# Tile 1's second attention: two pairs' scores and row maxima ahead of the last queries, the second eight experts behind the last pair, gates and first dots inside its end

## The reference

```python
logits = where(valid, q @ k.T / 8 + rel_bias, -1e30)        # 16 heads, 256 keys
probs  = softmax(concat([logits, sink]))[..., :-1]
x = x + (probs @ v) @ w_o
q  = (rmsnorm(x) @ w_q).reshape(tokens, 8, 2, 128)           # PEER: 8 heads, 2 halves
sv, si = top_k(q @ subkeys, 16)                              # of 128 keys, for each half
top_v, pos = top_k(sv[0][:, None] + sv[1][None, :], 16)      # 16 of 256 sums
g  = softmax(top_v);  e = index of the expert of each pos    # 128 experts a token
x = x + sum_e g_e * gelu(xn . u[e]) * v[e]
```

## Time and profile before

| | us |
|---|---|
| median of 3 runs (lowest, highest) | 1862.94 (1861.97, 1864.53) |
| time of the profiled execution | 1865.89 |
| its span, first to last instruction | 1863.7 |
| PE busy | 1628.6 |
| DVE busy | 1051.9 |
| POOL busy | 639.7 |
| ACT busy | 556.0 |

### The profile page before, as it was taken

How to read it: one execution, slowest core, us unless ns; L and a number is a source line. 1 busy time by engine, 2 the same in 40 slices (tenths; PEclk the granted TensorE clock), 3 DMA queues, 4 the chain that set the end, 5 groups by cost and what they waited for, 6 DMA issues and landing times.

```text
span 1863.7 us, 19396 instructions
## 1 busy us (share of the span) xinstructions
PE 1628.6 (87%) x6412; PEld 959.6 (51%) x6412; DVE 1051.9 (56%) x2710; ACT 556.0 (30%) x1673; POOL 639.7 (34%) x532
## 2 busy tenths in 40 slices
PE   9999999999997888888888789799888889877776
PEld 7888886976443444443443246554444444422222
DVE  3112202137656766666766654676676677676664
ACT  1211000102423333333333333433334333333432
POOL 1000000003534445344454530154444444444542
PEclk9999999999999999999999999999999999999999
DMA  9544238527999999999999995899999999999996
GB/s 250 137 120 164 101 136 302 183 91 300 415 415 421 421 421 421 414 410 417 422 418 406 421 352 205 315 402 415 418 421 421 421 421 417 422 416 418 417 419 285
DMA packets 153072, 642.57 MB, mean 345 GB/s; under 512 B 9987, under 2 KB 50067, under 8 KB 87180
## 3 DMA queue, kind: packets, MB, share of 16 engines
q0 software_dynamic: 74976, 540.92, 70.5%
q1 hardware_dynamic: 77996, 100.42, 16.2%
HBM read 640.19 MB, written 1.11 MB: 344 GB/s over the span
## 4 chain that ended last, share of the span: by engine, by line
PE 42%; DMA 37%; issue 7%; DVE 7%; ACT 4%; POOL 2%; SPq 1%; DVEq 0%; another core or an unknown queue 0%; POOLq 0%; ACTq 0%
DMA arena<-in_peer_uv,arena 35%; PE ps L1247 15%; PE ps L882 7%; PE ps L905 4%; DVE arena L1748 4%; POOL arena L585 2%; PE ps L1124 2%; PE ps L930 2%; PE ps L868 2%; PE ps L857 2%; ACT arena L737 1%; PE ps L1181 1%; ACT arena L732 1%; PE ps L1088 1%; PE ps L1080 1%
## 5 line engine op out<-in xcount | busy, mean ns | idle before, releaser
L1247 PE MATMUL ps<-arena 128*128 128x512 f32 x2048 | 960.4, 613 | 207.3 <-ACT arena L737 203.6
L585 POOL DMA_INDIRECT arena<-in_peer_uv,arena x512 | 628.4, 1227 | 1008.4 <-PE ps L1247 548.2
L1748 DVE CUSTOM_DVE_ANT_0 arena<-xn,arena 128x1024 f32<-128x1024 f32 x512 | 627.5, 1227 | 379.3 <-DMA arena<-in_peer_uv,arena 364.4
L1247 PEld LDWEIGHTS ps<-arena 128*128 128x128 f32 x2048 | 378.2, 194 | 730.4 <-issue 392.1
L727 ACT ACTIVATE arena<-arena 128x2 f32<-128x2 f32 x252 | 51.4, 204 | 803.0 <-DVE arena L1748 802.7
L737 ACT ACTIVATE arena<-const,arena 128x128 f32<-128x128 f32 x504 | 174.8, 394 | 8.2
L732 ACT ACTIVATE arena<-arena 128x1 f32<-128x1 f32 x504 | 121.3, 288 | 8.3
L882 PE MATMUL ps<-hT,wbuf 128*128 128x256 f32 x512 | 111.5, 379 | 1.0 <-DMA wbuf<-in_w_in 1.0
L882 PEld LDWEIGHTS ps<-hT,wbuf 128*128 128x128 f32 x512 | 96.9, 190 | 14.5 <-issue 1.3
L1124 PEld LDWEIGHTS ps<-hT,wbuf 128*128 128x128 f32 x736 | 89.2, 192 | 21.2 <-issue 21.2
L1124 PE MATMUL ps<-hT,wbuf 128*128 128x128 f32 x736 | 89.4, 275 | 0.0
(11 more groups left out here) (202 smaller groups left out, 1212.7 us busy)
## 6 DMA issues: line engine op xcount, KB each, us to landing
wbuf<-in_w_in SPq DMA_DIRECT2D x36, 512.0 KB, 6.8
wbuf<-in_w_in SPq DMA_DIRECT2D x7, 2048.0 KB, 8.6
wbuf<-in_peer_w_q SPq DMA_DIRECT2D x6, 2048.0 KB, 21.1
arena<-in_peer_uv,arena POOLq DMA_INDIRECT x512
wbuf<-in_conv_w_in SPq DMA_DIRECT2D x3, 2048.0 KB, 8.0
arena<-in_conv_w_in SPq DMA_DIRECT2D x3, 2048.0 KB, 17.8
wbuf<-in_attn_w_qkv SPq DMA_DIRECT2D x3, 2048.0 KB, 28.0
arena<-in_attn_w_o SPq DMA_DIRECT2D x3, 2048.0 KB, 15.5
```

The lines of the kernel that those rows point to most:

```text
L585: pool.indirect_dma_start(ring[:, e % RING], None, A["peer_uv"], bass.IndirectOffsetOnAxis(ap=expert[:, unit % 2, e:e + 1], axis=0))\
L1247: last = mm(ps[t][:, s * 512:(s + 1) * 512], diag[:, e % RING], ring[:, e % RING, D + s * 512:D + (s + 1) * 512], start=False, stop=False, ...
L1748: last = nc.vector.tensor_tensor_reduce(out=ring[:, e % RING, 0:D], in0=xn[:, v // PEER_HEADS], in1=ring[:, e % RING, 0:D], scale=1.0, sca ...
```

## The change

PE makes the scores of pairs 8 and 9 right behind the first keys, then the last attention queries, then the scores of pair 10, and the second part of the expert queries. The keys of that part go into the third pass of the attention's loop. ACT and DVE follow: ACT copies the second part's queries and scores in the second pass and exponentiates the gates in the third. DVE begins `attend(1)` right behind the first eight experts. The copy of the last attention queries goes behind the second pass, the search for places 9 to 16 behind the third, the work that turns these into experts behind the ninth, the gates behind the tenth and the first group's dots behind the eleventh, ahead of the last pair's copy. `w1` is no longer loaded; the first part reads the full 512 columns in wbuf 1, which are loaded before the output weights, and the output weights use wbuf 0 and wait for the attention queries' first half. The last query weights move to wbuf 0.

```diff
-FILLS = ([0] + [3] * 3 + [1] * 8, [3] * 4 + [1] * 10, [3] * 4 + [1] + [2] * 2 + [1] * 5)
+FILLS = ([0] + [3] * 3 + [1] * 9, [3] * 4 + [1] * 9, [3] * 4 + [1] + [2] * 2 + [1] * 5)
-QUERY_FILLS = ((None, (0, 9), (1, 10), (2, 9)), ((0, 11), (2, 11), (1, 13)))
+QUERY_FILLS = ((None, (0, 9), (1, 10), (2, 9)), ((1, 12), (2, 11), (0, 12)))
-KV_FILL, Q_FILLS, OUT_FILL = (1, 11), ((0, 10), (2, 10)), (1, 12)
+KV_FILL, Q_FILLS, OUT_FILL = (1, 11), ((0, 10), (2, 10)), (0, 11)
@@ sync @@
-            sp.dma_start(w1, cols(A["peer_w_q_2"][1], 0, 256)).then_inc(w1_landed, 16)
...
+            load(*QUERY_FILLS[1][0], cols(A["peer_w_q_2"][1], 0, 512))
             load(*OUT_FILL, cols(A["attn_w_o_2"], 0, 512))
-            for c in range(2):
-                load(*QUERY_FILLS[1][c], cols(A["peer_w_q_2"][1], c * 512, 512))
+            load(*QUERY_FILLS[1][1], cols(A["peer_w_q_2"][1], 512, 512))
@@ scalar, attend(t) @@
+                    if t == 1 and p == 1:
+                        queries_out(1, 1)
+                        scores_out(1, 1)
+                    if t == 1 and p == 2:
+                        softmax_exp(UNITS)
 
             attend(0)
...
-            for part in range(2):
-                queries_out(1, part)
-                scores_out(1, part)
-            softmax_exp(UNITS)
+            queries_out(1, 0)
+            scores_out(1, 0)
             attend(1)
@@ tensor @@
-                if layer and part == 0:
-                    pe.wait_ge(w1_landed, 16)
-                    return w1
...
-            def attend(t):
-                def scores_of(n):
+            def second_scores(n):
...
+            def attend(t, scored=0):
...
-                    if p < 8:
-                        scores_of(n)
+                    if scored <= p < 8:
+                        second_scores(n)
...
+                    if t == 1 and p == 2:
+                        keys(1, 1)
...
             keys(1, 0)
+            pe.wait_ge(q2_copied, 3)
+            second_scores(8)
+            second_scores(9)
             for j in range(4):
                 tile_queries(psD[:, 512:1024], 1, 1, j)
+            second_scores(10)
             query_part(1, 1, 2)
             query_part(1, 1, 3)
-            keys(1, 1)
             pe.wait_ge(q2_copied, 4)
-            attend(1)
+            attend(1, 3)
@@ vector @@
-                def first_experts(r):
-
-                    half, sel = slice(8 * r, 8 * r + 8), (sel_i, sel_j)
+                def first_places(r):
+
+                    half = slice(8 * r, 8 * r + 8)
                     if r:
                         linked(nc.vector.match_replace(cand, sel_v[:, 0:8], cand, LOWEST))
                     linked(nc.vector.max(sel_v[:, half], cand))
                     linked(nc.vector.max_index(sel_p[:, half], sel_v[:, half], cand))
+
+                def first_experts(r):
+
+                    half, sel = slice(8 * r, 8 * r + 8), (sel_i, sel_j)
...
+                def rest_of_places():
+
+                    first_places(1)
+                    first_largest()
+
+                first_places(0)
                 first_experts(0)
                 if layer:
-                    queries2_out(1, 1, psD)
-                first_experts(1)
-                first_largest()
-                if layer:
-                    attend(1)
+                    attend(1, {1: lambda: queries2_out(1, 1, psD), 2: rest_of_places, 8: lambda: first_experts(1), 9: lambda: gates(0), 10: lambda: dots(0, 0)})
                 else:
+                    rest_of_places()
+                    first_experts(1)
                     conv_late()
-                gates(0)
+                    gates(0)
                 for n in range(UNITS * UNIT_GROUPS):
...
-                    dots(v, g)
+                    if n or not layer:
+                        dots(v, g)
...
-            def attend(t):
+            def attend(t, between=None):
...
+                    if between and p in between:
+                        between[p]()
```

More of the change, by code:

```diff
@@ L279, in build @@
         wo2 = (at(4112, KC, 512), at(8208, KC, 512))
-        w1 = at(24320, KC, 256)
         qT = at(18464, KC, SEQ)
@@ L310, in build @@
         wo2_landed = sem("wo2_landed")
-        w1_landed = sem("w1_landed")
         gain_loaded = sem("gain_loaded")
@@ L1182, in out_step @@
                           skip_group_check=True)
-            def attend(t):
-                def scores_of(n):
[L1187 to L1194, removed]
+            def second_scores(n):
+                p, t = n % 8, n // 8
+                if n > 1:
+                    pe.wait_ge(max2_done, 2 * (n - 1))
+                for a in range(2):
+                    rows = slice(a * HD, (a + 1) * HD)
+                    last = mm(bank2(n, a)[:, 0:SEQ], qT[rows, p, t * P:(t + 1) * P], kT2[rows, p // 4], start=True, stop=True,
+                              skip_group_check=True)
+                last.then_inc(sc2_done, 1)
+            def attend(t, scored=0):
                 def turn_probs(n):
```

## The result

The changed kernel took 1865.86 us (median of 20 runs, 1863.88 to 1868.82), the kernel before 1864.01 in its 20 runs beside it (1861.76 to 1865.81): ratio 1.0013, 95% interval 1.0007 to 1.0019. By the ratio that is 2.4 us slower (the two medians lie 1.85 apart), where a gain of 1.2 us, to 1861.7, was forecast. 1865.86 is outside the range too; 1.1 us of that distance is not the change's, since the kernel before, 1862.94 where the forecast starts, stood at 1864.01 beside it. The loss is inside the 0.2% that the forecast called "same".

A forecast was written before the change was run, and what follows sets the result against it. The prediction took DMA's expert-layer pace (about 422 GB/s) as the bound, with 6.2 us recoverable. A 5.6 us gain at the last row maxima became 3.4 at the second weighted group, 1.2 after 2.2 for the clock: 1861.7 us, range 1858.7 to 1865.2.

The forecast's parts named there:

- pair 15 at 1191.4: DVE, end of the second attention: the last pair's row maxima start at 1191.4 instead of 1196.97, gaining 5.6 us.
- G: Mark the experiments count from: issue of the first of six gathers of expert rows by POOL in the second expert layer.
- R: Mark at the end of the second attention: start of the last pair's row maxima on DVE, forecast at 1191.4.
- S: The forecast's mark in the second expert layer: start of PE's second weighted group, 1211.25 before, forecast at 1210.0.
- R+16.4: Second weighted group on PE 16.4 us behind the last row maxima, against 14.3 before; without a clock cost, 3.4 us gained.
- 2.2 for the clock: PE at the clearing: a new idle gap of 3.3 us drops the clock to 0.5, costing 2.2 us (1.75 to 3.0).
- The clock rival: PE's clock doesn't fall in the new gap before the clearing, or recovers at once: gain 3.4 us, 1859.5; chance 0.20.
- The early gathers thus only move the hole: DMA, second expert layer: the hole at 1197 closes (2.7 us), but one of 2 us or more opens near 1208.
- 6.2 us: DMA time lost against 422 GB/s at the second expert layer's start, the most any edit here can return.
- The loads at zero: SP loads: exchanging the places of output weights and first query weights, equal in size, was costed at zero.
- What it gains, the end gains: Any gain at the start of PE's second weighted group reaches the kernel's end, up to 6.2 us.
- The stall rival: DVE's row maxima and normalising stall beside POOL's gathers at pairs 8 to 11: 1864.2, up to 1869.3; chance 0.17.

The follow-up runs named there:

- the loads run: Kernel before with only the change's loads and SP order, without w1: 1866.54 us, ratio 0.9993 to the kernel before.
- e1: Job on a chip that showed late signals; its trace of before is the kernel before repeated unchanged: 1867.28 us, ratio 0.9999.
- the filled run: Changed kernel with 12 and 24 unused 128-column matmuls in PE's two idle stretches at the attention's end: 1865.01 us, ratio 1.0006 to the kernel before.
- The two filled traces: Changed kernel with unused matmuls in PE's idle stretches, 64 or 36 of them: 1866.9 us (1.0019) and 1865.01 us (1.0006) against the kernel before.
- e3: Job on a chip without late signals; its trace of before is the kernel before repeated unchanged: 1863.84 us, ratio 1.0002.

## Why the prediction was wrong

**The step that failed** is the first term of the sum: "pair 15 at 1191.4. Before it was 1196.97, so 5.6 us are gained up to this point." The 1191.4 was right (1191.51, of which 0.4 is G's shift). The 1196.97 was that of one disturbed execution. R stood at G + 19.93 in it. In the kernel before's own trace without late signals it stands at 16.46, and in the run with gates and dots inside, whose order is the same up to R, at 15.18. So 3.5 to 4.75 of the 5.6 us weren't the order's: late signals of PE (the 1.21 and 1.32 us waits of the earlier trace rows) with the waits behind them, and a clock at 0.50 over 1185.7 to 1192.5. With a low stretch of 3.4 us and no late signal R came 1.3 us behind 15.18, with a late signal and the clock at 1.00 (the loads run) 1.4. The prediction saw the two waits, called them a possible stall of DVE, and used them only as a rival's price; it counted the end of the low stretch as a gain "inside the 5.6 us". It left both in the baseline as if they belonged to the order. The order itself gains 15.18 - 14.07 = 1.1 us at R, or 2.4 against the 16.46. Of three traces of the kernel before none had R at 15.18; all three had a low stretch there.

The sum again, at S, from the least disturbed traces of each order:

- before: R 15.18 + 14.28 (the forecast's trace) = G + 29.5. The version with two gathers first has 29.25, but the kernel before's own quietest trace has 30.64;
- pairs ahead of the last queries: -1.1;
- with gates and dots behind, S comes 16.00 us behind R instead of 14.28, +1.7. This is put down to the second eight experts' indices, now behind R; no run has that part alone;
- gates and dots inside: 31.42 - 30.08 = +1.3 (in before's order the same part costs 2.4 behind R);
- sum G + 31.4, which is 2.0 us later than before. Measured: 1.0013 and 1.0011, or 2.4 and 2.1 us.

That the two agree is partly luck. Between the kernels' own quiet traces (30.64; 31.40 and 31.42) S differs by only 0.8 us, and the rest behind S took 652.5 us against 652.9 and 653.8, so 0.4 to 1.3 us more are lost behind S. A place for it: over 375 to 410 us behind G, DMA moves 417 to 419 GB/s in five of the six traces of before's order (388 in e1's) and 384 to 410 in twelve of the thirteen of the changed one. No run shows why.

**The other steps.** "R+16.4" and 2.2 for the clock made R + 18.6; it was R + 17.3. The last copy came at R + 10.08 (R + 10.5 was said), the clearing at R + 10.4 (R + 10.8), the clock's cost was 1.67 by the filled run (1.75 to 3.0, 2.2 taken). So this part was a little too dear, and its sign right: the end of the attention loses 3 us against before's 14.28. The clock rival ("doesn't fall") didn't come: the clock was at 0.50 from 1198.5 to 1205.3, over the clearing. But it fell ahead of the gap of 2.94 us that was to bring it down, 1.5 us behind a gap of 1.76. The Trainium skill's "TensorE: Matmul & The Clock Gate", section "What's actually happening", has activity release the throttle. The two filled traces agree, with 1.00 throughout; but the same idle times of PE brought 0.50 in one trace with gates and dots behind and not in the other, so here idle times alone didn't decide it. "The early gathers thus only move the hole" held: 373 and 398 GB/s lie behind 1200.4. The "6.2 us" that any edit could return were 2.7 in an execution without late signals. The loads at zero: 0.9993, right. The SP load that goes out 1.1 us later is visible: over the first 4 us behind G DMA moves 250 to 282 GB/s in the changed order and 369 to 386 in before's (all traces in which the gathers aren't all held), 1 us of its time. Over the first 60 us behind G it is 397 and 394 GB/s in the changed kernel's quiet traces and 399 in e3's of before, 0.3 and 0.7 us of DMA's time, no more than the 0.8 by which S is later. So nothing speaks against the zero, though no run has it alone.

**"What it gains, the end gains"** held only roughly: the kernels with S at 31.4 to 31.8 in quiet traces have 1.0011 to 1.0013, those at 29.3 to 30.1 have 0.9997 to 1.0008. But three of the latter have an earlier S than the kernel before's 30.64 and yet ratios of 1.0004 to 1.0008, and the changed kernel with two gathers first has 1.0006 with S at 32.66. It can't be shown on single traces, since the rest behind S took 652.5 to 656.3 us in the three traces of before alone.

**The stall rival** named a place (pairs 8 to 11, the 7 us behind the first gather) and a size (up to 1869.3) that came true on one chip: S up to 6.7 us later than in a quiet trace, ratios 1.0036 and 1.0030. Its mechanism was wrong. DVE was not held beside POOL: its row maxima start 0.35 us apart as ever, and what comes late is PE's signal, to ACT first. So the port pair of the Trainium skill's "SBUF — State Buffer", section "SBUF: two separate sides", is not what these traces show. The change makes it worse, as I read the traces, because it puts a handshake of PE and ACT, on which the next row maximum hangs, 4.5 us behind G, where the signals can be held for 4 us; in the traces of before's order the longest wait for one is 2.3 us.

**Left open:** what holds PE's signals back, why on one chip (and once on the first), and why until 8.5 us. The runs show that it moves with the issue of the gathers, and that on the chip that has it one trace with two gathers first lacks the long wait at 4.5 us and the loss of 0.3% goes. (When that signal is due, four of the six are out.) They don't show the mechanism. How often it struck in the 20 timed runs of each kernel isn't known either.

## What to carry to other kernels

Before a baseline row becomes a term of a sum, ask whether its wait belongs to the order. A consumer that waits although its producer is done is a disturbance of that execution; take the time from the trace's steady pattern, or from a second trace, with it taken out. Compare the profiled execution's own time to its median first: 2.95 us above, as here, is more than the whole effect in question.

Work of an engine that is moved ahead of the copy on which the next stage hangs isn't hidden because the copy's data are late once; it has to fit the wait. Here 2.4 us of dots went into a gap of 0.85.

Where PE must be at full clock right behind a gap, a few unused products in it can keep the clock, as in the one trace here, if they end before the gap does. First see whether PE is what the next stage waits for: with gates and dots behind, half the clock at the clearing cost nothing.

## What the runs showed of the hardware

PE's completion signals can come up to 4.0 us behind the modelled end of its matmuls while it goes on to the next four, and while DVE's and ACT's signals pass (between the late ones at G + 5.74 and 8.62 in the forecast's trace). In all seven traces in which six gathers went out together and such a wait of over 1 us followed, the last of them ended 8.47 to 8.64 us behind the issue of the first gather; moving the gathers by 6.6 us, in one trace, moved it by as much.

PE fell to 0.50 of its clock at 1198.5 in the changed kernel, in its last product but ahead of its longest gap, and stayed there for 6.8 us. Filling its two gaps with 36 matmuls of 128 columns, 1.5 and 2.9 us, kept it at 1.00, and S came 1.67 us earlier.
